# Two-block transformer step on one core: the scan's inputs, its low-rank units and the later modulation dots move into the scan

## The reference, cut to what matters

```python
mod = (jax.nn.silu(c) @ ada_w[l] + ada_b[l])[:, None, :]
shift1, scale1, gate1, shift2, scale2, gate2 = jnp.split(mod, 6, axis=-1)
...
kk = hs(k * k_k)
kk = kk * lax.rsqrt(jnp.maximum(jnp.sum(kk * kk, axis=-1, keepdims=True), 1e-12))
for direction in range(2):
    w = -jax.nn.softplus(-(w_decay0[direction] + jnp.tanh(xw) @ w_decay_up[direction])) - 0.5
    decay = jnp.exp(-jnp.exp(w))
    a = jax.nn.sigmoid(a_gate0[direction] + xa @ a_gate_up[direction])
    k_dir = k * (1.0 + (a - 1.0) * k_a)
    ys.append(wkv7_scan(hs(r), hs(decay), hs(k_dir), hs(v), kk, hs(a), reverse=(direction == 1)))
```

## Time and profile before

| what | us |
|---|---|
| median of 3 runs | 2738.88 (2736.16 to 2738.94) |
| profiled execution | 2736.94 |
| its span, first to last instruction | 2735.1 |
| TensorE busy | 2327.1 (85%) |
| VectorE busy | 1576.7 (58%) |
| ScalarE busy | 1022.1 (37%) |
| GpSimd busy | 845.9 (31%) |
| mean granted TensorE clock | 0.952 of full |

### The profile page before, as it was taken

The page is one execution under the profiler, slowest core; times in us unless marked ns, Lnnn a source line. Parts: engine busy times, 40 slices in busy tenths (PEclk is TensorE's granted clock), DMA queues, the critical chain, the costliest instruction groups (busy, mean ns, idle before and its releaser), DMA issues. The chain is left out here.

```text
span 2735.1 us, 45574 instructions
## 1 busy us (share of the span) xinstructions
PE 2327.1 (85%) x17098; PEld 1389.2 (51%) x17098; DVE 1576.7 (58%) x3721; ACT 1022.1 (37%) x2631; POOL 845.9 (31%) x687
## 2 busy tenths in 40 slices
PE   7998799988999987777777777777789979889996
PEld 5775699956454432322232223322268878643333
DVE  5886765476656667676766667666554374420003
ACT  4535433343333333333333233333254233433333
POOL 0000211112444445555545554555500000123331
PEclk9998899999999999999999999999999956989998
DMA  8752200064999999999999999999922310389994
GB/s 312 294 198 108 90 4 5 25 241 181 395 392 383 383 388 421 420 422 419 414 417 414 413 416 415 415 414 417 408 96 78 111 38 2 138 328 370 366 362 163
DMA packets 156923, 771.19 MB, mean 282 GB/s; under 512 B 34192, under 2 KB 52256, under 8 KB 71200
## 3 DMA queue, kind: packets, MB, share of 16 engines
q0 software_dynamic: 87552, 545.34, 49.2%
q1 hardware_dynamic: 68144, 220.64, 21.3%
q10 hardware_dynamic: 1008, 2.29, 0.2%
HBM read 816.42 MB, written 16.78 MB: 305 GB/s over the span
## 5 line engine op out<-in xcount | busy, mean ns | idle before, releaser
L2243 PE MATMUL bank<-expert_rows,diagonals 128*128 128x512 f32 x1656 | 790.1, 616 | 206.5 <-ACT diagonals L2135 206.3
L2029 POOL DMA_INDIRECT expert_rows<-in_uv,expert_idx x414 | 528.8, 1277 | 581.9 <-PE bank L2243 488.3
L2064 DVE SCALAR_TENSOR_TENSOR expert_rows<-expert_rows,h_rows 128x1024 f32<-128x1024 f32 x414 | 507.6, 1226 | 347.8 <-DMA expert_rows<-in_uv,expert_idx 347.8
L2243 PEld LDWEIGHTS bank<-expert_rows,diagonals 128*128 128x128 f32 x1656 | 305.6, 194 | 638.5 <-ACT diagonals L2135 340.3
L2124 ACT ACTIVATE expert_act<-expert_dot 128x2 f32<-128x2 f32 x256 | 52.1, 203 | 868.9 <-DVE expert_rows L2064 660.5
L2243 PE MATMUL bank<-weight_slots,diagonals 128*128 128x512 f32 x392 | 184.1, 613 | 57.6 <-ACT diagonals L2135 57.6
L2135 ACT ACTIVATE diagonals<-ident,expert_weight 128x128 f32<-128x128 f32 x512 | 173.4, 385 | 0.0
L2064 DVE SCALAR_TENSOR_TENSOR weight_slots<-weight_slots,h_rows 128x1024 f32<-128x1024 f32 x98 | 120.0, 1225 | 89.9 <-DMA weight_slots<-in_uv,expert_idx 87.5
L2029 POOL DMA_INDIRECT weight_slots<-in_uv,expert_idx x98 | 131.1, 1338 | 113.1 <-issue 61.8
L2243 PEld LDWEIGHTS bank<-weight_slots,diagonals 128*128 128x128 f32 x392 | 71.8, 192 | 167.0 <-ACT diagonals L2135 88.1
L3562 DVE TENSOR_TENSOR hidden<-hidden,bank 128x256 f32<-128x256 f32 x24 | 10.1, 421 | 243.7 <-ACT hidden L3419 243.7
(11 more groups left out here) (566 smaller groups left out, 3951.1 us busy)
## 6 DMA issues: line engine op xcount, KB each, us to landing
expert_w<-in_experts SPq DMA_DIRECT2D x55, 1024.0 KB, 9.3
expert_w_more<-in_experts SPq DMA_DIRECT2D x41, 1024.0 KB, 8.7
mod_rows<-in_ada_rows SPq DMA_DIRECT2D x32, 1024.0 KB, 6.6
weight_slots<-in_w_in SPq DMA_DIRECT2D x8, 1536.0 KB, 7.0
mixed<-in_ada_rows SPq DMA_DIRECT2D x10, 1024.0 KB, 4.9
weight_slots<-in_w_in SPq DMA_DIRECT2D x4, 2048.0 KB, 10.1
weight_slots<-in_att_bias SPq DMA_DIRECT2D x8, 1024.0 KB, 7.6
weight_slots<-in_w_out SPq DMA_DIRECT2D x4, 2048.0 KB, 8.6
```

Of the source, the lines that this page charges most:

```text
L2029: pool.indirect_dma_start(rows[j], None, core.dram["uv"], bass.IndirectOffsetOnAxis(idx[:, t, column:column + 1], 0)).then_inc(arrived[j], 16)
L2064: dve.scalar_tensor_tensor(out=u, in0=u, scalar=1.0, in1=hN[:, t, :], op0=ALU.mult, op1=ALU.mult, accum_out=dot[:, j:j + 1]).then_inc(dott ...
L2243: mm = pe.matmul(bank[2 * (t % 2) + half][:, :], diag[:, j, :], rows[slot_of(n)][:, D + half * S:D + half * S + S], start=column == 0, sto ...
```

## The change

It has five parts.

1. Attention and the output projection lose their dots and the row loads for them, 8 dots with 4 rows and 18 dots with 9 rows. The call that adds the bias to the last columns stays at the projection's end.
2. The function `stage_rwkv_inputs` goes, with its 14 dots, and so one block of the program. Its other work stands in the scan's block: the key norms and the first 6 units ahead of round 0, units 6 and 7 after the second turn of round 0, and units 8 to 15 in round 0's levels 0 to 3.
3. The units are quadrant products. The two up-projections lie on partitions 0 to 63 and 64 to 127 of one unpadded tile, and four products of 64 rows and 64 columns make two units, the decay's and the rate's. The clearing of the padding by GpSimd goes. The sigmoid becomes ScalarE's tanh of half the argument and a correction on VectorE (`fix`, times 0.5 plus 0.5).
4. All 40 later dots stand in the scan: one at the end of each level in rounds 1 to 7 (35), and one after the gains in rounds 2 to 6 (5).
5. Their rows, the up-projections and their input lie in the memory of `x`, whose content isn't read in the scan. Two slots of 1 MB hold the rows; the first is loaded once all 16 units are raised. After the last dot SP loads x again (2 MB), waits for it, and only then comes to the loads of the next weights.

```diff
@@ stage_project (the output projection) @@
-        LATER_FIRST, LATER_LAST = 39, 48
-        LATER_AT = [2, 3, 4, 5, 6, 7, 8, 8, 9, 9, 10, 10, 11, 11, 13, 14, 14, 15]
-        if later is not None:
-            later_rows = core.sb("mod_rows", [P, 4, 2 * D], ctx=st)
-            later.lend(st, LATER_FIRST, LATER_LAST, [later_rows[:, i, :] for i in range(4)])
-                if later is not None:
-                    later.load_some(sp, LATER_FIRST, LATER_LAST)
-                    if later is not None:
-                        later.dot_some(dve, LATER_AT.count(i * KD + k))
@@ stage_attention @@
-        DOTS_AT = (6, 9, 12, 15, 18, 21, 25, 29)
-                m.load_some(sp, first_half, first_half + 2)
-                    if h < BIASES + 2:
-                        m.load(sp, first_half + 2 + h - BIASES)
-                    if u in DOTS_AT:
-                        m.dot_some(dve, 1)
@@ stage_rwkv_inputs: the whole function goes; of it @@
-        UNITS = [(d, f, which) for d in range(2) for f in range(4) for which in range(2)]
...
-                for u, (d, f, which) in enumerate(UNITS):
-                    if u >= NB:
-                        pe.wait_ge(emptied, u - NB + 1)
-                    pe.matmul(core.bank[u % NB][:, :], lora[:, which, d * S + f * P:d * S + f * P + P], low[:, :],
-                              start=True, stop=True).then_inc(bank_full, 1)
...
-                m.dot_some(dve, 2 * (LAST - FIRST))
@@ stage_rwkv_scan @@
+    UNITS, OPENING = 2 * ROUNDS, 6
+    M_FIRST, M_LAST = m.FIRST, m.QUARTERS // 2
+    units_of_level = lambda l: range(8 + 2 * l, min(10 + 2 * l, UNITS))
...
+        lora = core.x[:, 0:2, :].rearrange("p j t -> p (j t)")
+        low = core.x[:, 4, :]
+        sq = work[:, 14:18, :]
+        m.lend(st, M_FIRST, M_LAST, [core.x[:, 4 * i:4 * i + 4, :].rearrange("p k t -> p (k t)") for i in range(2)])
...
+                sp.wait_ge(unit_raised, UNITS)
+                m.load_some(sp, M_FIRST, M_LAST)
+                sp.wait_ge(m.dotted, 2 * M_LAST)
+                sp.dma_start(core.x[:, :, :], core.dram["xT"].rearrange("(k p) t -> p k t", p=P)).then_inc(x_reloaded, 16)
+                sp.wait_ge(x_reloaded, 16)
...
+                def fix(u):
+                    dve.wait_ge(unit_raised, u + 1)
+                    dve.tensor_scalar(rates_of_unit(u), rates_of_unit(u), 0.5, 0.5, ALU.mult, ALU.add).then_inc(fixed, 1)
...
+                        if n == 0 and l >= 1:
+                            for u in units_of_level(l - 1):
+                                fix(u)
...
+                        if n >= 1:
+                            m.dot_some(dve, 1)
                     add_y(n - 1)
                     gains(n)
+                    if 2 <= n < 7:
+                        m.dot_some(dve, 1)
...
+                def raise_unit(u):
+                    act.wait_ge(unit_full, u + 1)
+                    act.activation(rates_of_unit(u), unit_bank(u)[:, :], ACT.Tanh, scale=0.5,
+                                   bias=half_bias[:, u % 2, 4 * (u // 2 % 2) + u // 4:4 * (u // 2 % 2) + u // 4 + 1]).then_inc(unit_raised, 1)
...
+                def rate_units(u):
...
+                    for w, part in ((0, 0), (1, 1), (0, 1), (1, 0)):
+                        mm = pe.matmul(unit_bank(u + w)[half_rows(part), :], lora[half_rows(w), at + part * HD:at + part * HD + HD], low[half_rows(w), :],
+                                       start=True, stop=True)
+                    mm.then_inc(unit_full, 2)
...
+                        if n == 0 and units_of_level(l):
+                            if l == 0:
+                                pe.wait_ge(xs_out, 1)
+                            rate_units(units_of_level(l)[0])
```

More of the change, by code:

```diff
@@ L863, in stage_attention @@
     with ExitStack() as st:
-        rows = core.sb("mod_rows", [P, 2, 2 * D], ctx=st)
-        DOTS_AT = (6, 9, 12, 15, 18, 21, 25, 29)
-        first_half = m.FIRST
-        m.lend(st, first_half, first_half + len(DOTS_AT) // 2, [rows[:, i, :] for i in range(2)])
         score = core.sb("score", [P, SCORES, S], ctx=st)
@@ L1389, in _ @@
                 prelude(0, 4)
+                for f in range(1, PAIRS):
+                    scale_key(f)
+                for u in range(2, OPENING):
+                    fix(u)
                 for t in (tri[1], inv0[1], invT0[1]):
@@ L1400, in _ @@
                     chain(n - 1, 9)
+                    if n == 0:
+                        for u in range(OPENING, 8):
+                            fix(u)
                     for l in range(NL):
@@ L1514, in take_root @@
                     act.activation(rstd[f], rstd[f], ACT.Exp, scale=-0.5).then_inc(rooted, 1)
+                def raise_unit(u):
+                    act.wait_ge(unit_full, u + 1)
+                    act.activation(rates_of_unit(u), unit_bank(u)[:, :], ACT.Tanh, scale=0.5,
+                                   bias=half_bias[:, u % 2, 4 * (u // 2 % 2) + u // 4:4 * (u // 2 % 2) + u // 4 + 1]).then_inc(unit_raised, 1)
+                act.activation(low[0:HD, :], zr[0:HD, 12, :], ACT.Tanh).then_inc(squashed, 1)
+                act.activation(low[HD:P, :], zr[HD:P, 12, :], ACT.Copy).then_inc(squashed, 1)
+                for f in range(PAIRS):
+                    act.wait_ge(made, f + 1)
+                    act.activation(sq[:, f, :], kk[:, f, :], ACT.Square).then_inc(kk_squared, 1)
+                act.wait_ge(halved, 2)
+                for u in range(3):
+                    raise_unit(u)
+                act.wait_ge(clamped, 4)
+                act.activation(sq[:, :, :], sq[:, :, :], ACT.Ln).then_inc(kk_logged, 1)
+                act.wait_ge(kk_logged, 1)
+                for f in range(PAIRS):
+                    act.activation(sq[:, f, :], sq[:, f, :], ACT.Exp, scale=-0.5).then_inc(inverted, 1)
                 decays(0, 0)
+                raise_unit(3)
                 decays(0, 1)
+                for u in range(4, OPENING):
+                    raise_unit(u)
                 for n in range(ROUNDS):
@@ L1523, in _ @@
                         act.activation(to, bank[TURN_BANK[j]][:, :], ACT.Copy).then_inc(turn_out, 1)
+                        if n == 0 and j == 1:
+                            for u in range(OPENING, 8):
+                                raise_unit(u)
                     act.wait_ge(xs_full, n + 1)
@@ L1536, in _ @@
                                 act.activation(columns(invT[:, whole], m, late), compact(w_bank[h][:, 4 * RC:6 * RC], m), ACT.Copy).then_inc(w_out, 1)
+                        if n == 0:
+                            for u in units_of_level(l):
+                                raise_unit(u)
                         if l == 1 and rev_of(n):
@@ L1704, in _ @@
                         chain(n - 1, j)
+                        if n == 0 and j == 1:
+                            rate_units(OPENING)
+                    if n == 0:
+                        pe.wait_ge(unit_raised, 8)
                     for g in range(5):
@@ L1718, in _ @@
                             chain(n - 1, 11 + 2 * l)
+                    if n == 0:
+                        pe.wait_ge(unit_raised, UNITS)
                     end_products(n)
```

129 lines of the change are left out of this document (60 added, 69 removed).

## The result

| | before | after |
|---|---|---|
| median, us (runs) | 2738.87 (4) | 2756.49 (4) |
| lowest and highest, us | 2736.16, 2738.94 | 2752.35, 2756.89 |
| profiled execution, span | 2735.1 | 2755.0 |

The ratio is 1.0063, with a 95% interval of 1.0046 to 1.0081: the change makes the kernel slower by 17.6 us. 2729.4 was forecast, within 2718 to 2741.

What follows compares the result with a forecast made beforehand. TensorE was taken to bound attention and the scan's rounds, no engine the input stage between. Terms -10.0 - 11.5 + 12.0 = -9.5 us took the profiled 2736.9 to 2727.4; the median's 1.9 more gave 2729.4, range 2718 to 2741.

Steps and rivals of the forecast that it cites:

- Attention, -10.0: Attention without its 8 dots and 4 row loads: earlier bias load, full clock and one wait less save 10.0 us.
- The opening, -11.5: Start of the scan's block through round 0: earlier Gram banks, less the work moved into round 0, save 11.5 us.
- The first Gram bank's -15.8: Scan's opening: VectorE starts emptying the first Gram bank near 292.3 instead of 308.11, 15.8 us sooner.
- The dots in the rounds, +12.0: Scan rounds: 40 dots cost 12.0 us, nearly all behind level 0 and the gains, the rest hidden in idle time.
- The dots are on the path: Rival, scan rounds: every one of 40 dots costs its full 1.14 us, 45.6 instead of 12, time 2763; chance 0.09.
- Two row slots suffice: a row arrives in 5 to 7 us: Scan row loads: two slots are enough, as at least 8 us lie between a slot's second dot and next use.
- The chance of 0.09 for slower: Whole kernel: chance that the change is slower, the same 0.09 as the rival where every dot delays the rounds.
- Wrong if rounds grow by 5 us or more: Scan rounds, a sign of error: growth of 5 us, where about 2 (rounds 2 to 6) or 1 (1 and 7) was expected.

Runs made afterwards that it cites:

- e5_levels234: Kernel after with only the 21 scan dots behind levels 2, 3 and 4, those behind levels 0, 1 and the gains left out: 2723.4 us.
- e14_level1: Kernel after with only the seven scan dots behind level 1, the other thirty-three left out: 2730.8 us.
- e2_level0: Kernel after with only the seven scan dots behind level 0, the other thirty-three left out: median 2734.7 us, ten runs from 2722.6 to 2753.9.
- e6_loads: Kernel after without scan dots, but with all twenty rows of the scan loaded, spread evenly over rounds 1 to 7: 2755.7 us.
- e4_filler: Complete kernel after plus twelve products with unread results in TensorE's idle time in the rounds: 2740.2 us.
- e1_none: Kernel after without its forty scan dots and their row loads, x still reloaded: 2713.2 us.
- e11_after_paced_filler: Complete kernel after, its twenty rows each loaded in four successive transfers of 256 KB, plus twelve unread products in TensorE's idle time: 2785.9 us.
- e13_split_4: Kernel after with 22 dots in the scan and 18 back in the output projection; scan rows in four pieces, the first two whole: 2717.4 us.
- e9_loads_paced: Kernel after without scan dots, its twenty rows still loaded, evenly spread, each in four successive transfers of 256 KB: 2753.7 us.
- e3_gains: Kernel after with only the five scan dots behind the gains of rounds 2 to 6, the others left out: 2721.9 us.

## Why the prediction was wrong

- *Attention, -10.0*: right. The scan's block starts 9.6 us sooner, the bias waits are 1.57 and 1.99, the clock stays up to 250.
- *The opening, -11.5*: right, and a little low. The first Gram bank's -15.8 became -16.1 (29.6 instead of 45.7), and attention and opening together gave 23.2 by the end of round 0 against 21.5. Kappa ends 22.1 us behind the block's start (21.9 forecast), and a set of quadrant products among the levels takes 0.9 to 1.0 us of TensorE (1.02 counted).
- *The dots in the rounds, +12.0*: the direct delays and the places were right. Behind level 0 a dot costs 0.7 to 0.9 (0.95 forecast), behind level 1 nothing (0.1), behind levels 2 to 4 0.06 (0), behind the gains 0.6 to 0.8 alone and 0.9 in after (0.95 on average). By the higher figures of the single runs forty make 6.3 + 0 + 1.3 + 4.1, 11.7 us; in after the two waits are 9.4. "The dots are on the path" at a full 1.14 us each is refuted by e5_levels234 and e14_level1.
- **The step that failed** is that same sum, +12.0: it holds each dot's own delay and nothing else. Two terms in it were put at nothing.
- *The first missing term, and the larger one,* is the clock. I counted it in attention, where a stall of 4.11 us had brought it down, and left it out of the rounds, where my own sum put a stall of a microsecond into each. By the estimate it was 25.5 of the 40.3 us. Both kinds of stall are in it: e2_level0 fell with next to no traffic, e6_loads without dots, and fillers in the dots' gaps alone took away seven tenths of it (e4_filler, 7.2 left).
- *The second* is the loads: "Two row slots suffice: a row arrives in 5 to 7 us". I asked of the rows only whether they arrive in time, and priced twenty loads of 1 MB at nothing, since VectorE never waits for them. It doesn't. But TensorE stands while they pass, most likely for its instructions; evenly spread and alone, twenty of them cost 42 us (e6_loads against e1_none). In after the waits of this kind came to 3.6 us more than in e1_none, beside their share of the clock.
- What remains open: how after's 25.5 us divide between the two kinds. By the last wait ahead of each fall it is 15.4 behind the dots' stalls and 10.2 behind the others, in one profile. The effects don't simply add (e6_loads alone costs as much as the whole), and the kernel meant to tell it, e11_after_paced_filler, waited for its rows instead.
- The chance of 0.09 for slower stood on another mechanism, the dots' own length; no rival had the clock or the loads in the rounds. "Wrong if rounds grow by 5 us or more" was met: rounds 1 and 2 grew by 10.2 and 11.3.

## What to carry to other kernels

Before moving large transfers beside a stage in which TensorE runs many small instructions, look at its instruction transfers (here one of 16 KB per 3.8 us) in the view of the DMA queues; try the transfers in pieces, one behind the other, and check that the pieces still arrive when wanted. A stage in which TensorE is busy to 99% has more to lose from a stall than the stall's length: price a stall of a microsecond there with the low clock that can stand behind it, here 1.7 to 12 us for a fall. And work put into the idle time of an engine off the path is free only where the engine's next result isn't the one awaited: 28 of the 40 places here were free, and a version that uses 22 of them keeps the gain.

## What the runs showed of the hardware that I had not expected

- TensorE waiting with no releaser in the profile, for up to 2.9 us, in every kernel that loaded 1 or 2 MB at once during rounds 1 to 7; the instruction queue's transfers came some 2 us late at the places looked at (317.0, 320.5, 326.5 in e6_loads).
- The same bytes in transfers of 256 KB, one at a time: the longest such wait in rounds 2 to 7 is 0.5 us in e13_split_4 and 1.3 in e9_loads_paced, and the clock stays at 1.00 in both profiles. Each piece takes 3.5 us, so a row takes 14 us instead of 5.
- The lower clock in a stage where TensorE was busy to 97% (round 2 of after: 40.6 of 41.7 us, 11.3 longer than before), behind waits as short as 0.6 to 0.7 us; and the full clock kept behind one of 1.9 us (e3_gains). One and the same kernel (e2_level0) ran from 2722.6 to 2753.9 us.
- A kernel made faster by products that nobody reads (e4_filler against after, ratios to the kernel before of 1.0019 and 1.0063).
